# Two transformer blocks in float32r: every second weight chunk streamed in descending column order, and a scratch region moved by 32 bytes

## What is computed

```python
def reference(x, ...):
    x = first_block(x, ...)          # h + gla_mixer(rmsnorm(h)); h + mlp(rmsnorm(h)); rmsnorm
    return second_block(x, mem, ...) # h + hybrid_mixer; h + cross_attention; h + conv_ffn; rmsnorm

def _gla_mixer(h, w_in, ...):
    proj = h @ w_in                  # 2048 x 6160
    ...
    return (o * jax.nn.silu(r)) @ w_out

def _sq_relu_mlp(h, w_up, w_down):   # 2048 x 8192, 8192 x 2048
    a = jax.nn.relu(h @ w_up)
    return (a * a) @ w_down

def hybrid_mixer(xn, w_in, ...):
    proj = xn @ w_in                 # q, k, v of three branches, and three gates of 2048 columns
    ...                              # gated delta rule, sliding window, stick breaking
    merged = gate0 * (y_dn @ w_br_dn) + gate1 * (y_swa @ w_br_swa) + gate2 * (y_sb @ w_br_sb)
    return merged @ w_o

def conv_ffn(hn, w_up, ffn_conv, w_down):
    up = causal_dwconv(hn @ w_up, ffn_conv)
    gate, val = jnp.split(up, 2, axis=-1)
    return (jax.nn.silu(gate) * val) @ w_down
```

## Time and profile before

| | |
|---|---|
| median of two runs | 2684.03 us (2682.91 to 2685.15) |
| span of the profiled execution | 2683.7 us |
| PE busy | 2637.2 us, 98% of the span |
| PE weight loads busy | 2191.9 us, 82% |
| VectorE busy | 1458.2 us, 54% |
| ScalarE busy | 1150.4 us, 43% |
| mean granted TensorE clock | 0.994 |
| moved by DMA | 469.88 MB, 175 GB/s |

### The profile page before, as it was taken

The page is one execution under the profiler, slowest core; times in us unless marked ns, Lnnn a source line. Parts: engine busy times, 40 slices in busy tenths (PEclk is TensorE's granted clock), DMA queues, the critical chain, the costliest instruction groups (busy, mean ns, idle before and its releaser), DMA issues.

```text
span 2683.7 us, 31024 instructions
## 1 busy us (share of the span) xinstructions
PE 2637.2 (98%) x12560; PEld 2191.9 (82%) x12560; DVE 1458.2 (54%) x1101; ACT 1150.4 (43%) x1098; POOL 31.9 (1%) x36
## 2 busy tenths in 40 slices
PE   8999999999999999999999999999999899999997
PEld 6887888888888888788798888888888788878886
DVE  4544555545445445566765555454554566645665
ACT  4534444434334344454222344443364454444443
POOL 0000000000000000001000000000000000000000
PEclk9999999999999999999999999999999999999999
DMA  5454455555555555444223335555645355555555
GB/s 200 174 196 164 178 188 188 188 188 188 188 189 186 192 188 187 171 157 158 93 95 126 129 126 186 190 188 190 221 169 189 142 188 188 188 179 185 186 188 188
DMA packets 66725, 469.88 MB, mean 175 GB/s; under 512 B 7392, under 2 KB 7808, under 8 KB 10176
## 3 DMA queue, kind: packets, MB, share of 16 engines
q1 hardware_dynamic: 65536, 462.82, 48.0%
q0 software_dynamic: 1088, 5.55, 0.6%
HBM read 466.25 MB, written 2.10 MB: 175 GB/s over the span
## 4 chain that ended last, share of the span: by engine, by line
PE 76%; issue 20%; DVE 2%; ACT 1%; DMA 0%; POOL 0%; SPq 0%; POOLq 0%; DVEq 0%; ACTq 0%
PE acc L482 23%; PE acc L483 22%; PE acc L484 22%; PE tp L500 2%; PE tp L652 2%; PE tp L766 1%; DVE cv L1652 1%; DVE w_lo L1428 0%; PE tp L521 0%; PE tp L717 0%; ACT w_hi L1010 0%; PE tp L707 0%; ACT sw L1294 0%; ACT x_hi L1031 0%; DMA h<-in_x 0%
## 5 line engine op out<-in xcount | busy, mean ns | idle before, releaser
L1428 DVE TENSOR_TENSOR w_lo<-w_raw,w_hi 128x2048 fp32r<-128x2048 f32 x437 | 998.6, 2291 | 776.5 <-ACT w_hi L1010 775.6
L1010 ACT ACTIVATE w_hi<-w_raw 128x2048 fp32r<-128x2048 f32 x437 | 833.6, 1914 | 715.8 <-DMA w_raw<-in_stream 714.3
L482 PE MATMUL acc<-w_hi,x_hi 128*128 128x512 f32 (+1 forms) x2240 | 883.0, 394 | 10.8 <-DVE w_lo L1428 5.1
L484 PE MATMUL acc<-w_hi,x_lo 128*128 128x512 f32 (+1 forms) x2240 | 871.8, 389 | 0.0
L483 PE MATMUL acc<-w_lo,x_hi 128*128 128x512 f32 (+1 forms) x2240 | 871.5, 389 | 0.0
L482 PEld LDWEIGHTS acc<-w_hi,x_hi 128*128 128x128 f32 x2240 | 422.8, 189 | 100.7 <-issue 11.8
L484 PEld LDWEIGHTS acc<-w_hi,x_lo 128*128 128x128 f32 x2240 | 422.3, 189 | 87.4
L483 PEld LDWEIGHTS acc<-w_lo,x_hi 128*128 128x128 f32 x2240 | 422.9, 189 | 85.3 <-issue 1.7
L482 PE MATMUL acc<-w_hi,a_hi 128*128 128x512 f32 x1120 | 438.2, 391 | 2.4 <-DVE a_lo L1473 2.4
L484 PE MATMUL acc<-w_hi,a_lo 128*128 128x512 f32 x1120 | 436.6, 390 | 0.0
L483 PE MATMUL acc<-w_lo,a_hi 128*128 128x512 f32 x1120 | 436.4, 390 | 0.0
(11 more groups left out here) (337 smaller groups left out, 1315.8 us busy)
## 6 DMA issues: line engine op xcount, KB each, us to landing
w_raw<-in_stream SPq DMA_DIRECT2D x437, 1024.0 KB, 4.8
h<-in_x SPq DMA_DIRECT2D x4, 512.0 KB, 8.2
frow<-in_rows POOLq DMA_DIRECT2D x2, 1024.0 KB, 7.2
memt<-in_mem POOLq DMA_DIRECT2D x1, 2048.0 KB, 10.0
out_y<-h SPq DMA_DIRECT2D x4, 512.0 KB, 2.9
onorm<-in_rows POOLq DMA_DIRECT2D x1, 256.0 KB, 7.8
lvl<-in_masks POOLq DMA_DIRECT2D x1, 192.0 KB, 6.1
amask<-in_masks POOLq DMA_DIRECT2D x1, 192.0 KB, 2.7
```

Of the source, the lines that this page charges most:

```text
L482: pe.matmul(dst, xh, wh[:, k], start=first and k == 0, stop=False)
L484: mm = pe.matmul(dst, xl, wh[:, k], start=False, stop=last and k == n_k - 1)
L1010: act.activation(w_hi[:, c % SLOTS], w_raw[:, c % SLOTS], ACT.Copy).then_inc(hi_ready, 1)
L1428: dve.tensor_tensor(w_lo[:, c % SLOTS], w_raw[:, c % SLOTS], w_hi[:, c % SLOTS].bitcast(F32), ALU.subtract).then_inc(lo_ready, 1)
```

## The change

In `chunk`, where the number of the chunk is odd, the moving operand and the result are given as reversed views: the weights are read from the last column to the first, and the sums are written from the last column to the first. Column j of the weights still meets column j of the sum, so the result is the same. The stationary operand is read as before. Every loop over chunks has an even number of chunks a turn and starts at an even chunk, so "odd" is the same set in each turn. Apart from this, the cursor is rounded up to a multiple of 128 before `a_s` is taken: `a_s` and `a_z` begin 32 bytes later, `a_s` at 175488. The number and the order of the instructions on every engine are those of before.

```diff
@@ -78,6 +78,7 @@
         rstd = sb("rstd", [P, 8, M])
         rhalf = sb("rhalf", [P, 8, M])
         mhalf = sb("mhalf", [P, M * 8])
+        cursor[0] = (cursor[0] + 127) // 128 * 128
         a_s = take(48 * K)
         a_z = take(9 * K // 2)
         assert cursor[0] <= nc.sbuf_usable_end, (cursor[0], nc.sbuf_usable_end)
@@ -479,9 +480,12 @@
                         xh = lhs[0][:, k0 + k, m * P:(m + 1) * P]
                         xl = lhs[1][:, k0 + k, m * P:(m + 1) * P]
                         dst = acc[:, blk % 2, m, 0:width]
-                        pe.matmul(dst, xh, wh[:, k], start=first and k == 0, stop=False)
-                        pe.matmul(dst, xh, wl[:, k], start=False, stop=False)
-                        mm = pe.matmul(dst, xl, wh[:, k], start=False, stop=last and k == n_k - 1)
+                        w1, w2 = wh[:, k], wl[:, k]
+                        if c % 2:
+                            dst, w1, w2 = dst[:, ::-1], w1[:, ::-1], w2[:, ::-1]
+                        pe.matmul(dst, xh, w1, start=first and k == 0, stop=False)
+                        pe.matmul(dst, xh, w2, start=False, stop=False)
+                        mm = pe.matmul(dst, xl, w1, start=False, stop=last and k == n_k - 1)
                 mm.then_inc(used, 1)
```

## The result

The changed kernel takes 2711.32 us, the median of two runs (2710.8 and 2711.83), against 2684.03 us before. The ratio is 1.0102, with a 95% interval of 1.0073 to 1.0132: 27.3 us slower. That is under the 2% within which a measurement of this kernel was said to show no change, but the interval leaves 1 out, and a gain of 2.6 us was forecast.

What follows compares the result with a forecast made beforehand. PE was taken to bound the kernel by the distance between matmul starts. Span 2683.7 - 2.6 (region) + 0 (order) = 2681.1 us, as a median 2681.5 us; own range 2679 to 2685, 8-in-10 range 2612 to 2718 us.

Steps and rivals of the forecast that it cites:

- The bound: PE's matmul stream: the distance between starts, 226.6 ns per 512 columns, 2349 us or 88% of the span.
- The region term: Chunks against m_hi and m_lo: aligning the stationary operand saves 6.7 ns on each of 384 matmuls, 2.6 us.
- The order term: The 5,232 matmuls of odd chunks: descending order costs 0, bounded by 68 us gained and 200 ns more each.
- The rival of 2716 us: Odd chunks: descending streams start at an unaligned address and pay 6.7 ns a matmul, 35 us; chance 0.10.
- The half rate: Odd chunks: descending columns are not paired, 427 ns between starts, 1046 us more, 3728 us; chance 0.11.
- the charge per 128 columns: Odd chunks: moving operand pays 6.7 ns per 128 columns, 26.8 ns a matmul, 140 us, 2822 us; chance 0.07.
- The vanished charge: Odd chunks: opposite read directions part two meeting reads, removing 13 ns a matmul, 68 us, 2613 us; chance 0.07.

Runs made afterwards that it cites:

- e1: Kernel before with only the region moved (cursor rounded up to a multiple of 128), all chunks ascending: 2680.64 us, ratio 0.9987.
- e9: All chunks ascending; both weight halves of slots 0 to 3 offset 0, 32, 64, 128 bytes from agreement modulo 256 with the stationary operands: 2719.71 us.
- e4: Full change without the region move: odd chunks descend, cursor line left out: 2714.04 us, ratio 1.0117.
- e2: Full change, but in odd chunks only the weights are read descending, sums written ascending; region moved: 2711.57 us, ratio 1.0106.
- e3: Full change, but in odd chunks only the sums are written descending, weights read ascending; region moved: 2680.78 us, ratio 0.9991.
- e5: Full change with even chunks descending as well, so all chunks descend; region moved: 2742.95 us, ratio 1.0223.
- e6: Kernel before, all ascending, region unmoved; slots 0 to 3 of w_hi begin 0, 16, 32, 60 bytes behind a multiple of 64: 2720.63 us.
- e7: All chunks descending, region as before; slots 0 to 3 of w_hi begin 0, 4, 32, 36 bytes behind a multiple of 64: 2755.26 us.
- e10: All chunks descending; both weight halves of slots 0 to 3 offset 0, 32, 64, 128 bytes from agreement modulo 256 with the stationary operands: 2748.0 us.
- e11: Full change, with 96 of 128 stationary columns in all matmuls except those opening and closing a sum: 2734.27 us.

## Why the prediction was wrong

**The bound** was read rightly: PE, by the distance between starts, nothing covering it. (Besides the first and the last slice of the earlier trace rows one more, the 32nd, shows an 8; nothing hangs on it.) A loss of 6.67 ns a matmul went into the time nearly in full, and the busy time of no other engine moved by more than 1 us.

**The region term** was right in mechanism and size: 2.6 us computed, 2.7 measured in e1. The rule cited there, that weight loading takes nothing from the running matmul (the Trainium skill, "TensorE: Matmul & The Clock Gate", Part 2), is not borne out in this kernel. In e1 and e9, where all reads ascend and the width is the same, the distance is 226.7 ns or up to 8 ns more, by the places of the operands alone. The reading "a charge for an operand off by 32 bytes" was too simple. It is a matter of the two operands together (e9), and in the changed kernel half of the 2.6 us was not to be had, since odd chunks have 233.3 ns at either place of `m_hi` (e4). The prediction said that only that address differed between the rows; the stage differed too, and it was e1 that showed the address to be the cause.

**The order term** is the step that failed: "Between these ends I take 0, the value of the nearest row." It is 6.67 ns a matmul, 33.3 us for the 4,992 matmuls outside the stage of `m_hi`, on the read side alone (e2, e3). The argument was about which bytes are touched. But the prediction had already found 13 ns per matmul that exist only at the full rate, and a further 6.7 ns that hang on an address. It even noted that this "reads as a charge for fetching operands". Such a charge is a reason to expect that the sequence of fetches matters. With it in hand, 0 should not have had 0.65. The runs bear out the observation itself: at the lower clock neither direction nor address moves the 427 ns (e5).

**The rival of 2716 us** had the price (6.7 ns a matmul) and came within 5.2 us of the time, but for a mechanism that fell: e6 and e7 show that an unaligned start is neither needed nor enough. The half rate and the charge per 128 columns did not occur: 233.3 ns, not 427 or 253. Descending writes cost nothing (e3). So the rule of the Trainium skill ("PSUM — Partial Sum Buffer", Specifications), that a non-contiguous pattern slows matmuls significantly, has no hold on a step of minus one: 226.67 ns. The vanished charge did not occur either. But its argument, two reads that meet, is the nearest to what the runs show. It was given 0.07 only, because the 226.6 ns were the same for "different pairs of addresses". They were not different in what counts: `w_hi` (65664), `w_lo` (32896), `x_hi` (98432), `x_lo`, `a_hi` and `a_lo` all agree modulo 256, `m_hi` at 175456 does not, and at 175488 it does.

**What is shown, and what is open.** Shown: at the higher clock the spacing of float32r matmuls of 512 columns depends on the direction of the moving read, on the difference of the addresses of the moving and the stationary operand, and on the width of the stationary one. The kernel before stands at the best of the combinations tried (226.67 ns). Descending reads never settled under 233 ns: 233.3 ns is their distance in most places, with 235.6 to 236.7 ns in some slots of e7 and e10 and some chunks of e11. They cost 6.67 ns here because before was at that best point; at other places an ascending read is as dear or dearer. Not explained: that the same addresses give 233.3 ns in some chunks and 236.7 in others (e10, e11). Argued, not shown: that the two reads disturb each other inside the chip in a repeating rhythm. A direct test would read the stationary operand in the opposite order as well; this was not tried.

## What to carry to other kernels

Where matmuls follow each other without a gap, read the distance between their starts, by operand, and compare groups that should be equal; a difference of 3% is a place for a gain or a trap. For float32r streams of 512 columns, try first what was best here: operands at addresses that agree modulo 256, read ascending. (In e1 `m_hi` lies 256 bytes off the others modulo 512 and stands at 226.67 ns; 128 bytes off was not enough in e9.) And when a trace shows a small regular charge whose cause is unknown, give an edit that touches its surroundings a real chance to move it, even if the bytes stay the same.

## What the runs showed of the hardware

- Descending writes into PSUM (step -1, 512 columns) cost nothing: 226.67 ns (e3).
- Descending reads of 256 columns are a little faster than ascending ones, 118.3 against 120.0 ns; of 512 columns they are slower, 233.3 against 226.7 ns.
- Ascending reads with the weights 32 bytes off, in the narrow chunk 241 of e9, stand at 116.6 ns, under the 120.0 ns of before. Which place is best depends on the width.
- At the lower clock level (1.2 GHz) 512 columns take 427 ns, ascending or descending (e5), at every difference of addresses that met it (e6 to e10).
- At the higher level one stream at fixed addresses can run at 233.3 or at 236.7 ns (e10, offset 128: 38 and 66 chunks).
